# P-V products of four head kinds computed transposed, two heads side by side

## The reference

```python
p = masked_softmax(s, kpos[None, :] <= t[:, None])          # fox; sel and win of nsa likewise
o = jnp.einsum('bhts,bshd->bthd', p.astype(v.dtype), v)     # the P-V product
...
a = jnp.where(strict, jnp.exp(jax.nn.log_sigmoid(z) + suffix), 0.0)            # stick: no division
...
return (g[..., 0:1] * o_cmp + g[..., 1:2] * o_sel + g[..., 2:3] * o_win).astype(q.dtype)    # nsa
```

## Time and profile before

| what | value |
|---|---|
| median of three runs | 1566.98 us |
| profiled execution, span from first to last instruction | 1562.3 us |
| TensorE busy (matmuls) | 1449.2 us, 93% |
| VectorE busy | 471.9 us, 30% |
| ScalarE busy | 197.7 us, 13% |
| DMA: 481.6 MB in the span | 308 GB/s |

### The profile page before, as it was taken

How to read it: one execution, slowest core, us unless ns; L and a number is a source line. 1 busy time by engine, 2 the same in 40 slices (tenths; PEclk the granted TensorE clock), 3 DMA queues, 4 the chain that set the end, 5 groups by cost and what they waited for, 6 DMA issues and landing times.

```text
span 1562.3 us, 16829 instructions
## 1 busy us (share of the span) xinstructions
PE 1449.2 (93%) x6928; PEld 710.3 (45%) x6928; DVE 471.9 (30%) x939; ACT 197.7 (13%) x427; POOL 2.5 (0%) x23
## 2 busy tenths in 40 slices
PE   5899899999999999977989999999999999998886
PEld 2575665555544757652424333434243334332232
DVE  4478735345334555360100011112120110110101
ACT  1123223000003132330000000000000001000000
POOL 0000000000000000000000000000000000000000
PEclk9999889999999999989999999999999999999999
DMA  9945425886874310049999999999999999999995
GB/s 345 362 141 212 168 106 197 270 305 237 311 279 168 109 55 1 1 184 409 419 413 418 409 419 405 407 411 418 413 416 409 416 405 411 412 409 419 417 401 224
DMA packets 151647, 481.60 MB, mean 308 GB/s; under 512 B 15848, under 2 KB 33640, under 8 KB 144144
## 3 DMA queue, kind: packets, MB, share of 16 engines
q1 hardware_dynamic: 150120, 478.64, 79.0%
q10 hardware_dynamic: 1448, 1.84, 0.4%
HBM read 479.41 MB, written 1.06 MB: 308 GB/s over the span
## 4 chain that ended last, share of the span: by engine, by line
PE 74%; DMA 17%; DVE 4%; SPq 2%; ACT 1%; issue 1%; DVEq 0%; ACTq 0%
PE bank L1608 24%; PE bank L1644 13%; DMA ring<-in_moe_wu 13%; PE bank L1480 9%; PE bank L1202 6%; PE bank L1498 5%; PE bank L1444 3%; PE bank L1191 2%; DMA ring<-in_moe_wg 2%; DMA ring<-in_ada_w 1%; DVE ada_acc L1742 1%; PE bank L1293 1%; SPq L780 1%; PE bank L1545 1%; PE bank L1362 1%
## 5 line engine op out<-in xcount | busy, mean ns | idle before, releaser
L1608 PE MATMUL bank<-ring,h_T 128*32 128x512 f32 (+1 forms) x2240 | 307.6, 609 | 49.8 <-DMA ring<-in_moe_wu 38.0
L1644 PE MATMUL bank<-ring,m_qk_T 128*32 128x512 f32 (+2 forms) x1344 | 250.1, 601 | 10.6 <-issue 9.6
L1608 PEld LDWEIGHTS bank<-ring,h_T 128*32 128x32 f32 (+1 forms) x2240 | 97.6, 118 | 246.4 <-issue 245.3
L1608 PE MATMUL bank<-ring,cmp_region 128*128 128x512 f32 x448 | 196.3, 592 | 1.2 <-DVE m_s_region L2338 1.2
L1644 PEld LDWEIGHTS bank<-ring,m_qk_T 128*32 128x32 f32 (+2 forms) x1344 | 90.0, 129 | 166.5 <-issue 166.5
L1480 PE MATMUL bank<-ring,h_T 128*128 128x384 f32 (+1 forms) x448 | 156.8, 503 | 0.7 <-DVE m_s_region L2137 0.7
L1608 PEld LDWEIGHTS bank<-ring,cmp_region 128*128 128x128 f32 x448 | 84.1, 190 | 102.0 <-issue 102.0
L1202 PE MATMUL bank<-ring,h_T 128*128 128x512 f32 (+1 forms) x320 | 116.1, 512 | 0.8 <-ACT wide L887 0.5
L1480 PEld LDWEIGHTS bank<-ring,h_T 128*128 128x128 f32 x448 | 83.3, 190 | 61.3 <-issue 15.5
L1034 ACT ACTIVATE m_qk_T<-bank 128x512 f32<-128x512 f32 x35 | 20.9, 597 | 656.5 <-PE bank L1624 656.0
L2338 DVE SCALAR_TENSOR_TENSOR m_s_region<-m_s_region,bank 128x512 f32<-128x512 f32 x35 | 24.1, 688 | 263.9 <-PE bank L1608 263.9
(11 more groups left out here) (347 smaller groups left out, 1007.3 us busy)
## 6 DMA issues: line engine op xcount, KB each, us to landing
ring<-in_moe_wg SPq DMA_DIRECT2D x56, 2048.0 KB, 20.9
ring<-in_moe_wu SPq DMA_DIRECT2D x56, 2048.0 KB, 20.2
ring<-in_moe_wd SPq DMA_DIRECT2D x54, 2048.0 KB, 22.8
ring<-in_ada_w SPq DMA_DIRECT2D x28, 1024.0 KB, 8.8
ring<-in_ada_w SPq DMA_DIRECT2D x10, 2048.0 KB, 14.1
ring<-in_w_in SPq DMA_DIRECT2D x10, 2048.0 KB, 10.7
ring<-in_ffn_wg SPq DMA_DIRECT2D x6, 1536.0 KB, 10.2
ring<-in_ffn_wu SPq DMA_DIRECT2D x6, 1536.0 KB, 8.9
```

Of the source, the lines that this page charges most:

```text
L1608: last = mm(b[c0:c1, :], xT[st.team % 2][:, k, c0:c1], w, start=k == 0, stop=k == KC - 1)
L1644: last = mm(ps[half][c0:c1, :], hbT[:, unit, 128 * q + c0:128 * q + c1], down_at(slot, 512)[:, q, 512 * half:512 * half + 512], start=st.b ...
```

## The change

- The exponentials of sel, win and fox heads are divided and gated before they are turned. ScalarE takes the logarithm of the row sum (for nsa times 1 + exp(-g), the inverse of the gate, for which `nsa_gates` loses its reciprocal), the exponential of its negative, and two copies of the exponentials scaled by that column.
- `third_two(i)` multiplies two heads in one step in every odd slot from 3 on, except for mlstm: V is the stationary operand (64 columns), the turned weights move (256 columns for the first key tile, 128 for the second), and the two heads' outputs lie in partitions 0 to 63 and 64 to 127 of bank 4 (stick: bank 5). The output has the dimensions on the partitions, as `wout` needs it. `prob_T` gets a third buffer.
- sel, win and the compressed product accumulate in one bank. `cmp_out` moves from the end of slot 3 to ahead of its P-V, `cmp_turned` ahead of the third convolution.
- `finish` remains for mlstm alone. `take` copies the bank of nsa (slot 9), fox (slot 17) and stick (slot 21, in two parts) to `mixT`, which lies in the memory of `x_norm`. Only mlstm's outputs are transposed (slot 16).
- `wout(1, 1, ...)` does its third pair in slot 20.

```diff
@@ -173,8 +173,12 @@
             dve("part1", s)
             if HEADS[s][0] != "stick":
                 act("exp", s)
-        if s >= 2:
+        if s == 3:
+            pe("cmp_out")
+        if s >= 2 and s - 2 < NH and HEADS[s - 2][0] == "mlstm":
             pe("third", s - 2)
+        elif s >= 3 and s % 2:
+            pe("third_two", s - 3)
         if s < len(fill):
             proj(fill[s][0], *fill[s][1:])
         if s == 0:
...
@@ -190,14 +194,11 @@
         elif s == 2:
             pe("cmp_turn")
+            dve("cmp_turned")
             dve("conv", 2)
-            dve("cmp_turned")
         elif s == 3:
-            pe("cmp_out")
             dve("conv", 3)
-            dve("cmp_take")
         elif s == 5:
-            dve("finish", 0)
...
@@ -206,7 +207,7 @@
         elif s == 9:
-            dve("finish", 1)
+            dve("take", "nsa")
...
@@ -216,33 +217,26 @@
         elif s == 13:
-            dve("finish", 2)
+            dve("finish")
         elif s == 16:
-            pe("mix_T", 0)
-            act("mix_cols", 0)
-            pe("mix_T", 1)
-            dve("mix_cols", 1)
+            pe("mix_T")
+            dve("mix_cols")
         elif s == 17:
-            dve("finish", 3)
+            dve("take", "fox")
             pe("wout", 0, 0, (0, 1))
         elif s == 18:
-            pe("mix_T", 2)
-            act("mix_cols", 2)
             pe("wout", 1, 0, (0, 1))
         elif s == 19:
             pe("wout", 0, 1, (0, 1, 2))
         elif s == 20:
-            pe("wout", 1, 1, (0, 1))
+            pe("wout", 1, 1, (0, 1, 2))
         elif s == 21:
+            dve("take", "stick")
             pe("wout", 0, 0, (2,))
-            dve("finish", 4)
             pe("wout", 1, 0, (2,))
-            pe("mix_T", 3)
-            dve("mix_cols", 3)
-            pe("wout", 1, 1, (2,))
...
-        mix = xn
+        mixT = xn[:, :, :].rearrange("p t (k n) -> p t k n", k=KC)
-        probTs = [probT[:, 0, :], probT[:, 1, :]]
+        probTs = [probT[:, 0, :], probT[:, 1, :], cmp_region[:, 4 * S:4 * S + 384]]
...
@@ -954,17 +947,16 @@
                         return
                     for tt, (a, b) in enumerate(((0, 128), (128, 384))):
                         do(act.activation(e[:, a:b], e[:, a:b], ACT.Exp, bias=nmax[:, i % 4, tt:tt + 1],
-                                          accum_out=lsum[:, i // H, h, tt:tt + 1]), head_exp if tt else None)
+                                          accum_out=lsum[:, i // H, h, tt:tt + 1]))
+                    for tt in range(TT):
+                        part = 1.0 if kind == "fox" else ng[:, tt, 3 * h + (1 if kind == "sel" else 2):3 * h + (2 if kind == "sel" else 3)]
+                        do(act.activation(rl[:, h, tt:tt + 1], lsum[:, i // H, h, tt:tt + 1], ACT.Ln, scale=part))
+                    do(act.activation(rl[:, h, :], rl[:, h, :], ACT.Exp, scale=-1.0))
+                    for tt, (a, b) in enumerate(((0, 128), (128, 384))):
+                        do(act.activation(e[:, a:b], e[:, a:b], ACT.Copy, scale=rl[:, h, tt:tt + 1]), head_exp if tt else None)
                 does = {"evac": evac, "gate_ln": gate_logs, "gates_exp": gate_exps, "rstd": rstds, "tanh": tanhs, "cmp_exp": compressed_exp,
...
@@ -1338,31 +1330,42 @@
+                def third_two(i):
+                    kind, h = HEADS[i]
+                    if kind == "stick":
+                        pe.wait_ge(stick_exp, N_STICK * l + h + 2)
+                    else:
+                        pe.wait_ge(head_pT, N_P * l + count(PKINDS, i + 1))
+                    if h == 0:
+                        if kind in ("fox", "stick"):
+                            pe.wait_ge(o_free, 4 * l + 2)
+                        pe.wait_ge(proj_evac, NG * l + 1 + NTH[{"fox": (3, 1), "stick": (5, 1)}.get(kind, (6, 2))])
+                    for tt in range(TT):
+                        for q in range(2):
+                            if kind in ("fox", "stick"):
+                                v = (fv if kind == "fox" else sv)[:, tt, DH * (h + q):DH * (h + q) + DH]
+                            else:
+                                v = nv[:, tt, int(kind == "win"), :]
+                            o = turned_out(kind)[DH * q:DH * q + DH, 128 * h + 128 * tt:128 * h + 256]
+                            last = mm(o, v, probTs[(i + q) % 3][:, 256 * tt:256 + 128 * tt], start=h == tt == 0 and kind in ("fox", "stick"),
+                                      stop=tt == 1 and kind != "sel", skip_group_check=True)
+                            if tt:
+                                last.then_inc(head_pv, 1)
...
                 def cmp_product():
                     pe.wait_ge(cmp_pT_evac, l + 1)
-                    for tt in range(TT):
-                        last = mm(ps[2][:, 256 * tt:256 * tt + 256], pcT[:, tt, :], vblk[:, :, :].rearrange("p h d -> p (h d)"),
-                                  start=True, stop=True)
-                    last.then_inc(cmp_out, 1)
-                def mix_transposes(j):
-                    pe.wait_ge(mix_ready, 4 * l + j + 1)
...
+                def mix_transposes():
+                    pe.wait_ge(mlstm_mixed, l + 1)
+                    pe.wait_ge(proj_evac, NG * (l + 1))
+                    for k in range(2):
                         for tt in range(TT):
+                            last = nc.tensor.transpose(ps[7][:, 256 * k + 128 * tt:256 * k + 128 * tt + 128], mo[:, tt, 128 * k:128 * k + 128], ident)
                     last.then_inc(mixT_done, 1)
...
@@ -1950,9 +1946,9 @@
-                    e, b, pt = probs[i % 2], ps[HEAD_BANK[i]][:, 0:384], probTs[i % 2]
-                    if i >= 2:
-                        dve.wait_ge(head_pv, NH * l + i - 1)
+                    e, b, pt = probs[i % 2], ps[HEAD_BANK[i]][:, 0:384], probTs[i % 3]
+                    if i >= 3:
+                        dve.wait_ge(head_pv, NH * l + i - 2)
...
@@ -1963,46 +1959,31 @@
+                def take(kind):
+                    dve.wait_ge(head_pv, NH * l + {"nsa": 2 * H, "fox": 4 * H, "stick": 5 * H}[kind])
+                    k = {"nsa": 6, "fox": 2, "stick": 4}[kind]
+                    o = turned_out(kind)[:, :].rearrange("p (a t n) -> p t a n", a=2, t=TT)
                     if kind == "stick":
                         for tt in range(TT):
+                            do(V.tensor_copy(mixT[:, tt, k:k + 2, :], o[:, tt]), mixT_vec)
+                    else:
+                        do(V.tensor_copy(mixT[:, :, k:k + 2, :], o), mixT_vec)
+                    do.also(o_free)
```

More of the change, by code:

```diff
@@ L674, in ada_bank, with mlstm_out, turned_out @@
             return ps[6 + c % 2] if (l, c // 4) == (0, 0) else ps[2] if l == 0 and 5 <= c < 10 else ps[3] if (l == 0) == (c < 10) else ps[7]
[L676 to L680, removed]
+        def mlstm_out(tt):
+            return ps[4 + tt][:, 0:H * (DH + 1)]
+        def turned_out(kind):
+            return ps[5 if kind == "stick" else 4]
         block = ctx.enter_context(nc.Block())
@@ L944, in stick_weights @@
                     act.wait_ge(stick_shift, N_STICK * l + HEADS[i][1] + 1)
-                    do(act.activation(probTs[i % 2], probTs[i % 2], ACT.Exp), stick_exp)
+                    do(act.activation(probTs[i % 3], probTs[i % 3], ACT.Exp), stick_exp)
                 def head_exps(i):
@@ L1459, in mixer @@
                         "nsa_T": nsa_transposes, "kv_T": kv_transposes, "cmp_scores": compressed_scores, "cmp_turn": cmp_turn,
-                        "cmp_out": cmp_product, "fox_T": fox_transposes, "first": first, "first_two": first_two, "minima": minima, "second": second, "third": third,
+                        "cmp_out": cmp_product, "fox_T": fox_transposes, "first": first, "first_two": first_two, "minima": minima, "second": second, "third": third, "third_two": third_two,
                         "mix_T": mix_transposes, "wout": wout}
@@ L1964, in part2 @@
                         do(V.tensor_copy(pt, b), head_pT)
-                def finish(gi):
-                    kind = HEADS[H * gi][0]
-                    dve.wait_ge(head_pv, NH * l + H * gi + H)
-                    o = [outputs(gi, tt) for tt in range(TT)]
-                    cols = {"mlstm": 0, "fox": 256, "stick": 512}.get(kind, 768)
-                    dst = [mix[:, tt, cols:cols + 256].rearrange("p (h d) -> p h d", h=H) for tt in range(TT)]
-                    if kind == "mlstm":
-                        for tt in range(TT):
-                            ov = o[tt].rearrange("p (h d) -> p h d", h=H)
-                            dn = small[:, 8:12]
-                            do(V.tensor_copy(dn.rearrange("p (h o) -> p h o", o=1), ov[:, :, DH:DH + 1]))
-                            do(STT(dn, dn, -1.0, dn, ALU.mult, ALU.max))
-                            do(TTop(dn, dn, expnm[:, tt, :], ALU.max))
-                            do(V.reciprocal(dn, dn))
-                            do(TTop(mh[:, tt, :, :], ov[:, :, 0:DH], bc(dn, DH), ALU.mult), o_free if tt else None)
```

(22 more changed lines are left out.)

109 lines of the change are left out of this document (29 added, 80 removed).

## The result

The changed kernel took 1582.30 us (median of 4 runs, 1581.95 to 1585.75) against 1568.38 for the kernel before beside it (4 runs, 1563.69 to 1570.24). The ratio is 1.0103, 95% interval 1.0082 to 1.0124: slower, by 13.9 us in the medians and by 16 as the ratio has it. The forecast was 1576.5 us, +9.5. Between the two profiled executions the span grew from 1562.3 to 1580.1, +17.8. This is more than the medians show: the changed kernel's profiled execution took 1581.95 us for its span of 1580.1, and 1.9 us on top of 1562.3 makes the profiled execution of the kernel before a quick one of its kind, some 3 us under its median (an estimate). Of the later kernels e6 and e10 have one run each in a slow state (1775.28 and 3000.97 us), which is left out of their times and ratios.

What follows compares the result with a forecast made beforehand. TensorE's order of work was taken as the bound. Layer 1 (6.1 + 2.5 - 2.0 = +6.6) and layer 0 (+2.9) gave +9.5 on the 1562.3 us span; median forecast 1576.5, own range 1572 to 1583, overall 1564 to 1590.

Steps and rivals of the forecast that it cites:

- Part 1: Division and gate on ScalarE: five dependent instructions (the link) between exponential and turning, 1.85 us per nsa head, 1.67 fox.
- the ring: Turning, VectorE copy, next logits, ScalarE exponential, next turning: 3.85 us hidden by TensorE's list, becoming 5.7 for nsa.
- Layer 0: First layer's mixer: +4.7 through slot 8, +0.2 in the fox slots, -2.0 behind; total +2.9 us.
- Layer 1 up to slot 8: Turnings of slots 2 to 8 take 5.75 us more, slot 2's is 1.1 late: +6.8 at slot 8.
- Layer 1's end: From slot 17, where TensorE's list bounds again, fewer products and transposes save 2.0 us.
- rival (a): New gaps in slots 4 to 8 of both layers drop TensorE to 1.2 GHz: +15, 1591 us; chance 0.15.
- Part 2: Paired products side by side take 0.86 us, saving about 0.5 a pair, worth nothing in slots 2 to 15.
- (d): Product halves don't run side by side, 0.65 us more in four pairs per layer: +5, 1582 us; chance 0.05.
- (b): The ring stays covered, added ScalarE work under about 1 us, TensorE saves 10 us: 1557 us; chance 0.08.
- (c): Partly covered, added ScalarE work of 1.3 us, savings and waits near balance: 1570 us; chance 0.16.
- (e): ScalarE table reloads between logarithm, exponential and copy, 1.28 us each: over 1620 us; chance 0.02.
- Part 3: VectorE's lost finishes, new takes and third probT buffer, beside TensorE's projections: worth 0 us.

Runs made afterwards that it cites:

- e6: Changed kernel with VectorE's next-head logits ahead of the copy in slots 1 to 15 and the last fox product in slot 16: 1567.30 us, ratio 1.0013.
- e10: e9 with the reciprocal of sel and win heads' sums on VectorE instead of ScalarE's logarithms and exponential: 1580.77 us, ratio 1.0096.
- e1: Changed kernel without the five added ScalarE instructions, so output not divided or gated: 1734.22 us, only the mixers comparable.
- e3: Changed kernel with VectorE's logits and maxima of the next head ahead of the copy of turned weights, slots 1 to 15: 1572.77 us, ratio 1.0043.
- e5: Kernel before the change with e3's edit, logits ahead of the copy in slots 1 to 15: 1565.08 us, ratio 0.9997.
- e4: Changed kernel with the product of the last two fox heads issued in slot 16 instead of 17: 1576.83 us, ratio 1.0074.
- e7: e6 with ScalarE's tanh and its table loads moved from slot 6 to slot 5: 1571.42 us, ratio 1.0037.
- e9: e6 with the products of heads 0 to 5 issued in slots 4, 6 and 8: 1564.5 us, ratio 0.9992.
- e2: Kernel before with only division and gate moved to ScalarE, products and transposes as they were: 1587.53 us, ratio 1.0124.
- e8: Kernel before with fox head 14's product issued in slot 17 instead of 16: 1565.69 us, ratio 1.0007.

## Why the prediction was right, and where its sizes were off

**Part 1: right.** Priced 1.85 us; the chain has 566.47 to 568.33, 1.86, in five instructions of 0.30, 0.30, 0.21, 0.41 and 0.52. The copies in the groups by form on ScalarE, 80 to 702 us (busy us, mean ns):

```profile
L956 ACT ACTIVATE prob<-prob,inv_sums 128x256 f32<-128x256 f32 x24 | 12.2, 507 | 0.8
L956 ACT ACTIVATE prob<-prob,inv_sums 128x128 f32<-128x128 f32 x24 | 9.6, 402 | 0.8
```

The copies at 507 and 402 ns lie on the line of the earlier trace rows; of the small ones L953 takes 294 and L954 203 in this view, against 295 and 203 there. That the ring binds at 5.7 a turn is shown by the chain, by e1 and, best, by e3 against e5.

**Layer 0: right up to the last fox head; the end is in part the clock's.** Turning of slot 2: +1.5 (priced +1.1). Slots 2 to 8: +5.5 (priced +4.5), the rest from slot 7, where pair and projection ran at half clock:

```profile
132.74 1.19 PE bank L1365 x8
133.92 4.89 PE bank L1194 x8
```

Last fox head: 196.58 against 190.25, +6.3, forecast 4.7 + 1.6. The end then takes back 4.0, forecast 3.4 (1.4 in the fox slots, 2.0 behind). Sum +2.3 for +2.9. How much of the 4.0 is the work that was removed isn't shown: over this end the kernel before had a clock of 0.50 from 192 to 204, the changed one only from 204 to 207, with 0.55 and 0.82 beside it. That this term came out so near is partly luck.

**Layer 1 up to slot 8: the slot terms held.** +8.7 from 579.62 to 590.61, less layer 0's 2.3, against +6.8; the difference is the projection at 569.73, which took 5.33 instead of 3.49. That is no fixed cost: in e4, which is the same kernel up to slot 15 and waited the same 1.76 us ahead of this turning, the projection took 3.63. The fox heads add 2.8 (forecast 2.5).

**Layer 1's end: the failed term.** "Sum -2.0 per layer", counted from slot 17, took it as free that head 14's product and nsa's four transposes leave slot 16. They were TensorE's work inside the wait of the stick-breaking chain. Without them the output projection and its neighbours ran at 1.2 GHz: from slot 16's turning to the projection's end +2.6 instead of -2.0, and e4 (alone) and e6 (against e3) give back 4.5 and 4.7 us by their ratios. A further 1.3 us is the router's matmul (L1114), 3.27 us for 1.97, again at 1.2 GHz:

```profile
693.00:696.00 3.00, 2.66 (x13) 0.50 0.00 0
```

It takes 3.1 to 3.6 in e1, e3, e4, e6, e7 and e9 too, and 1.97 to 2.15 in e2, e5 and e8, which have the old products. So it goes with the changed products and their outputs and not with the link; by which step was not tried. So the excess of 8.2 us in layer 1 is 1.8 (slot 5), 4.6 (slots 16 to 18) and 1.3, and 0.5 in smaller differences.

Falls of the clock stood in the prediction as rival (a), with a chance of 0.15, but in the wrong place: "some six new gaps of 1.2 to 1.7 us in slots 4 to 8". Of these, in the profiled execution, one in each layer lowered the clock (slot 7 of layer 0, slot 5 of layer 1). The wait that did most was an old one that a removed product had helped to fill. The section HAM oscillation of the Trainium skill's page "TensorE: Matmul & The Clock Gate" says that gaps between groups of matmuls can throttle the engine anew each time. The trace agrees for these two and for slot 16 and doesn't for most slots of the same form.

**Part 2: the price was right, the saving less than half.** Priced 0.86 and a saving of 0.5 a pair; the product takes 0.80, but the group behind it 0.14 more, and e1's slots 2 to 8 show some 0.2 a pair in layer 0 and under 0.1 in layer 1. As 0.80 lies far from the 1.5 without overlap, the halves do run side by side, and (d) falls, though its 1582 us is the number that came out. The Trainium skill ("TensorEngine Tiling (Array Packing)", section When to Use Tiling) advises this very swap with two column tiles for a streamed operand 64 wide. The trace agrees that the two halves overlap. In this kernel the swap came with the division ahead of the product, and that put 1.86 us on the ring.

**(b) and (c)** needed a shorter link; it was 1.86. **(e)**: no table load stands between the five instructions.

**Part 3: right.** No wait of TensorE on a take shows. What I missed there is in the order: VectorE's copy ahead of the logits was free before (e5) and is 0.59 us of each turn of the ring now.

**The sum.** The prediction is right in the direction and in its main cause: the link, at its price, on a ring that became the bound. The measured 1582.30 us lies at the upper end of the forecast's own range. What brought it there is the clock behind slot 16 and ahead of the router, which the sum had at nothing.

## What to carry to other kernels

Before work is moved from one engine to another, write down the ring beside the busiest engine's list and the distance between the two: the same 0.59 us a slot on VectorE is worth 9.4 us where the ring binds and nothing where it doesn't. An instruction placed in a queue costs what stands behind it while it waits (e7, e10), not its duration. And work removed from beside a wait isn't free for TensorE: look whether what is left keeps its clock, and if it doesn't, move something small into the gap before anything else.

## What the hardware showed that I had not expected

- A gap decides the clock only loosely. At slot 16 of layer 1 (e2 apart) waits of 1.98 to 2.42 us were followed by 1.2 GHz in four profiles of four, waits of 1.31 in none of two, and waits of 1.6 in two of five and then for a shorter time. In slot 5 the same wait of 1.76 us was followed by 1.2 GHz in the changed kernel and not in e4.
- One such fall costs more than the gap: 0.8 us of matmuls moved by one slot gave 4.5 us (e4).
- A group of full-width matmuls (eight of 512 columns) took 3.63 us at full clock where it followed matmuls on a part of the array: the column-half pair, the stick-breaking scores with 64 rows (start 658.56 in the changed kernel), mLSTM's minima with 4 rows (141.63). Behind full-width products it took 3.49, and 3.44 behind transposes. It does so also where nothing waits (e1).
